# Two-layer hybrid block on one NeuronCore: last expert units one by one, scatter and output by column parts, ten constant products ahead of the ranks

## The reference

```python
g_sel = argmax(xt @ wg + bg)                       # 1 of 4 groups
top_v, top_i = top_k(e_logits[g_sel], 2)           # 2 of its 8 experts
gates = softmax(top_v) * g_gate
...
y[token] += gate * ((silu(xb @ w1[e]) * (xb @ w3[e])) @ w2[e])     # for each chosen expert e of 32
```

## Time and profile before

| | |
|---|---|
| median of 3 runs | 1458.95 us (1457.89 to 1459.53) |
| the profiled execution's own time | 1456.56 us |
| its span | 1454.7 us, 14458 instructions |
| TensorE products busy | 1142.2 us (79%) |
| VectorE, ScalarE, GpSimd busy | 326.3, 198.2, 43.7 us |
| moved by DMA | 477.99 MB, mean 329 GB/s |
| granted clock, mean | 0.909 of full speed |

### The profile page before, as it was taken

One profiled execution on the slowest core, in us unless ns is written; L12 is line 12 of the kernel. 1 busy time (PEld: TensorE's weight loads), 2 busy tenths in 40 slices (PEclk: granted clock), 3 DMA queues, 4 the chain that ended last, 5 costly groups with the idle time before them and its releaser, 6 DMA issues.

```text
span 1454.7 us, 14458 instructions
## 1 busy us (share of the span) xinstructions
PE 1142.2 (79%) x5962; PEld 563.6 (39%) x5962; DVE 326.3 (22%) x843; ACT 198.2 (14%) x468; POOL 43.7 (3%) x79
## 2 busy tenths in 40 slices
PE   8999998977768766685869999998866666666575
PEld 5775455543223222231325776465312212122121
DVE  1216543132021110110102286232201101011011
ACT  2024302210000010000002252131000000000000
POOL 0110000000000000000001100000000000000000
PEclk9999999979889898997989999998988888789888
DMA  9663373369999999999998355534999999999996
GB/s 368 217 232 116 114 284 123 116 243 418 426 425 428 427 423 427 427 427 425 428 409 319 116 174 207 199 116 173 403 427 428 426 427 426 427 427 428 427 427 264
DMA packets 94356, 477.99 MB, mean 329 GB/s; under 512 B 6390, under 2 KB 15054, under 8 KB 44878
## 3 DMA queue, kind: packets, MB, share of 16 engines
q1 hardware_dynamic: 93367, 475.25, 80.7%
...
...
## 4 chain that ended last, share of the span: by engine, by line
PE 54%; DMA 37%; DVE 4%; SPq 1%; ACT 1%; issue 1%; POOL 0%; DVEq 0%; ACTq 0%; POOLq 0%
PE bank L1445 51%; DMA ring<-exp_w 36%; PE bank L1452 2%; SPq L563 1%; DMA conv_mem<-memT 1%; DMA ring<-w_in 1%; ACT fox_ssd L746 0%; DVE SCO L1029 0%; DVE fox_ssd L1193 0%; DVE X L1038 0%; ACT H L897 0%; DVE proj_ht L976 0%; ACT SCO L742 0%; DVE proj_ht L997 0%; DVE Y L1284 0%
## 5 line engine op out<-in xcount | busy, mean ns | idle before, releaser
L1445 PE MATMUL bank<-ring,proj_ht 128*32 128x512 f32 (+3 forms) x2496 | 455.0, 673 | 153.4 <-DMA ring<-exp_w 150.8
L1445 PEld LDWEIGHTS bank<-ring,proj_ht 128*32 128x32 f32 (+1 forms) x2496 | 170.4, 142 | 393.8 <-issue 380.9
L1445 PE MATMUL bank<-ring,SCO 128*32 128x512 f32 x928 | 128.8, 690 | 67.4 <-DMA ring<-exp_w 58.4
L1038 DVE TENSOR_TENSOR X<-X,bank 128x512 f32<-128x512 f32 x64 | 44.0, 688 | 310.0 <-PE bank L1445 310.0
L1445 PE MATMUL bank<-ring,H 128*128 128x512 f32 x256 | 112.5, 593 | 0.0
L1445 PE MATMUL bank<-proj_ht,H 128*128 128x128 f32 x512 | 77.1, 304 | 28.4 <-DVE proj_ht L997 25.9
L1445 PEld LDWEIGHTS bank<-proj_ht,H 128*128 128x128 f32 x512 | 67.5, 209 | 67.3 <-DVE proj_ht L997 36.9
L1445 PEld LDWEIGHTS bank<-ring,SCO 128*32 128x32 f32 x928 | 35.4, 124 | 145.9 <-issue 133.6
L1029 DVE SCALAR_TENSOR_TENSOR SCO<-Y,bank 128x512 f32<-128x512 f32 x16 | 17.1, 1069 | 289.6 <-PE bank L1445 289.6
L1445 PE MATMUL bank<-fox_ssd,proj_ht 128*128 128x512 f32 x128 | 59.1, 604 | 17.8 <-ACT fox_ssd L746 17.8
L1445 PEld LDWEIGHTS bank<-ring,H 128*128 128x128 f32 x256 | 47.7, 190 | 55.6 <-issue 55.0
...
## 6 DMA issues: line engine op xcount, KB each, us to landing
ring<-exp_w SPq DMA_DIRECT2D x182, 2048.0 KB, 19.9
ring<-w_in SPq DMA_DIRECT2D x8, 2048.0 KB, 17.3
ring<-xa_wkv SPq DMA_DIRECT2D x4, 2048.0 KB, 10.0
ring<-w_out SPq DMA_DIRECT2D x4, 2048.0 KB, 9.5
ring<-xa_wq SPq DMA_DIRECT2D x4, 2048.0 KB, 9.6
ring<-xa_wo SPq DMA_DIRECT2D x4, 2048.0 KB, 7.7
ahead<-xa_wkv SPq DMA_DIRECT2D x4, 2048.0 KB, 28.1
...
```

The lines of the kernel that those rows point to most:

```text
L1038: last = v.tensor_tensor(x, x, bank[B_SCAT[i]][:, :], ALU.add)
L1445: return nc.tensor.matmul(dst, lhsT, rhs, start=start, stop=stop)
```

## The change

1. The host lays the 268 columns of `fv` out as one contiguous array `w_fv`; one load takes the place of two (the second brought the 8 columns of dt in pieces of 32 bytes).
2. Channel `c * 128 + p` of X now belongs to partition `p`, chunk `c` (before, channel `8 * p + c`), so that a chunk is a run of 128 columns. `w_in`, `xa_wq` and `xa_wkv` are read with that row order, and gains and the transposed memory are laid out by it. The input of the experts and router keeps the old order.
3. HT of layer input is made by column parts: parts of both tiles for columns 0 to 511, then 512 to 1023; banks 5 and 6 change places.
4. Ten products `ident` x `tri` of 256 columns go into the ranks' bank after the logits, in both layers; nobody reads them.
5. Down products of units 10 and 11: first all of column half 0, then half 1. In the last quad of a layer unit 10 is waited for and used alone, then unit 11. ScalarE copies each half when it is done.
6. Scatter and sums: half 0 of both tiles, then half 1, each with its own semaphore step. The output goes in four pieces of 128x512 instead of two of 128x1024.

```diff
@@ -121,7 +120,7 @@
-    jobs = two("hT1", 0) + two("hT1", 1)
+    jobs = [("hT1", t, i) for i in range(2) for t in range(NT)]
@@ -158,7 +157,7 @@
-PINNED = {("hT1", 0, 0): 2, ("hT1", 0, 1): 5, ("hT1", 1, 0): 6, ("hT1", 1, 1): 7, ("rank",): 5, ("total",): 7}
+PINNED = {("hT1", 0, 0): 2, ("hT1", 1, 0): 5, ("hT1", 0, 1): 6, ("hT1", 1, 1): 7, ("rank",): 5, ("total",): 7}
@@ -197,10 +196,12 @@
+N_IDLE = 10
...
+SCATTER = [(t, c) for c in range(2) for t in range(NT)]
@@ -444,6 +444,10 @@
+        def added(s, n, t, c):
+            return s.x_added, n * len(SCATTER) + SCATTER.index((t, c)) + 1
@@ -522,9 +526,9 @@
-                w = W_FV if kind == "fv" else w
-                rows = "(c p) n -> p c n" if kind in ("w_out", "wo") else "(p c) n -> p c n"
-                v = a[name][l].rearrange(rows, c=KC)
+                if kind == "fv":
+                    return w, a["w_fv"][l].rearrange("p (c n) -> p c n", c=KC)
+                v = a[name][l].rearrange("(c p) n -> p c n", c=KC)
@@ -542,11 +546,7 @@
-                place = ring_view(i % SLOTS, IN_COLS["fv"][1] if unit[0] == "fv" else w)
-                sp.dma_start(place[:, :, 0:w], src).then_inc(landed[i % SLOTS], 16)
-                if unit[0] == "fv":
-                    dt = a["w_in"][l].rearrange("(p c) n -> p c n", c=KC)[:, :, C_DT:C_DT + SH]
-                    sp.dma_start(place[:, :, w:], dt).then_inc(dt_in, 16)
+                sp.dma_start(ring_view(i % SLOTS, w), src).then_inc(landed[i % SLOTS], 16)
@@ -636,12 +636,13 @@
-            for t in range(NT):
-                sp.wait_ge(first.x_added, (DEPTH * NQ - 1) * NT + t + 1)
+            for t, c in SCATTER:
+                sp.wait_ge(*added(first, DEPTH * NQ - 1, t, c))
...
-                sp.dma_start(out[0, t * P:(t + 1) * P, :], X[:, t, :]).then_inc(x_out, 16)
-            sp.wait_ge(x_out, 16 * NT)
+                cols = slice(c * 512, (c + 1) * 512)
+                sp.dma_start(out[0, t * P:(t + 1) * P, cols], X[:, t, cols]).then_inc(x_out, 16)
+            sp.wait_ge(x_out, 16 * len(SCATTER))
@@ -741,10 +742,12 @@
-                act.wait_ge(*used(s, n, 12))
-                for i in range(2):
-                    last = nc.scalar.copy(YS[:, i * 512:(i + 1) * 512], bank[B_DOWN[i]][:, :])
-                last.then_inc(s.YS_ready, 1)
+                for c in range(2):
+                    if c == 0:
+                        act.wait_ge(s.down_half, n + 1)
+                    else:
+                        act.wait_ge(*used(s, n, MOE_UNITS))
+                    nc.scalar.copy(YS[:, c * 512:(c + 1) * 512], bank[B_DOWN[c]][:, :]).then_inc(s.YS_ready, 1)
@@ -1031,15 +1034,12 @@
-                for i in range(4):
-                    t, c = i // 2, i % 2
+                for i, (t, c) in enumerate(SCATTER):
...
-                    last = v.tensor_tensor(x, x, bank[B_SCAT[i]][:, :], ALU.add)
-                    if c == 1:
-                        last.then_inc(s.x_added, 1)
-                dve.wait_ge(s.x_added, n * NT + NT)
+                    v.tensor_tensor(x, x, bank[B_SCAT[i]][:, :], ALU.add).then_inc(s.x_added, 1)
+                dve.wait_ge(s.x_added, n * 4 + 4)
@@ -1052,8 +1052,9 @@
-                for t in range(NT):
-                    transposed_x("hT1", g_ch[:, G_X, :], t)
+                for i in range(2):
+                    for t in range(NT):
+                        gained(l, ("hT1", t, i), g_ch[:, G_X, 4 * i:4 * i + 4], HT[:, t, 4 * i:4 * i + 4, :])
@@ -1547,21 +1546,43 @@
-                for i in range(4):
-                    if i % 2 == 0:
-                        u = landed_rows(2, i // 2, 1024)
+                def down(u, experts, i, c):
+                    for e in experts:
+                        r = slice(CAP * e, CAP * (e + 1))
+                        last = mm(bank[B_DOWN[c]][r, :], HIDT[:, i, r],
+                                  u[e // 2][:, e % 2, i % 2, c * 512:(c + 1) * 512], start=i == 0, stop=i == 3)
+                    return last
+                u = landed_rows(2, 0, 1024)
+                for i in range(2):
...
-                        for e in range(QUAD):
-                            r = slice(CAP * e, CAP * (e + 1))
-                            last = mm(bank[B_DOWN[c]][r, :], HIDT[:, i, r],
-                                      u[e // 2][:, e % 2, i % 2, c * 512:(c + 1) * 512], start=i == 0, stop=i == 3)
-                    if i % 2 == 1:
-                        last.then_inc(s.units_used, 2)
+                        last = down(u, range(QUAD), i, c)
+                last.then_inc(s.units_used, 2)
+                if s is first and q == NQ - 1:
+                    u = []
+                    for pair in range(2):
+                        u.append(landed_unit(10 + pair, 1024))
+                        for c in range(2):
+                            for i in (2, 3):
+                                last = down(u, (2 * pair, 2 * pair + 1), i, c)
+                            if pair == 1 and c == 0:
+                                last.then_inc(s.down_half, 1)
+                        last.then_inc(s.units_used, 1)
+                else:
+                    u = landed_rows(2, 1, 1024)
+                    for c in range(2):
+                        for i in (2, 3):
+                            last = down(u, range(QUAD), i, c)
+                        if c == 0:
+                            last.then_inc(s.down_half, 1)
+                    last.then_inc(s.units_used, 2)
...
-                pe.wait_ge(s.YS_ready, n + 1)
-                for i in range(4):
-                    t, c = i // 2, i % 2
+                for i, (t, c) in enumerate(SCATTER):
+                    pe.wait_ge(s.YS_ready, n * 2 + c + 1)
@@ -1572,16 +1593,17 @@
-                def transpose_x(name, t):
-                    for i in range(2):
-                        transposes(l, (name, t, i), [dealt(t)[:, 4 * i + j, :] for j in range(4)])
-                for t in range(NT):
-                    if l == 0:
-                        pe.wait_ge(x_in[t], 16)
-                    else:
-                        pe.wait_ge(first.x_added, (l * NQ - 1) * NT + t + 1)
-                    transpose_x("hT1", t)
+                def transpose_x(name, t, i):
+                    chunks = [slice((4 * i + j) * P, (4 * i + j + 1) * P) for j in range(4)]
+                    transposes(l, (name, t, i), [X[:, t, c] for c in chunks])
+                for i in range(2):
+                    for t in range(NT):
+                        if l == 0:
+                            pe.wait_ge(x_in[t], 16)
+                        else:
+                            pe.wait_ge(*added(first, l * NQ - 1, t, i))
+                        transpose_x("hT1", t, i)
@@ -1837,17 +1865,20 @@
-                transpose_x("xT", 0)
+                transpose_dealt_x(0)
...
-                transpose_x("xT", 1)
+                transpose_dealt_x(1)
...
+                pe.wait_ge(*free(l, job))
+                for _ in range(N_IDLE):
+                    mm(bk(l, job)[:, 0:S], ident, tri[:, 0:S])
...
-                pe.wait_ge(*free(l, job))
@@ -1911,11 +1942,13 @@
-    gains = np.stack([g["norm1_g"], g["mem_norm_g"], g["norm2_g"]], axis=1).reshape(DEPTH, 3, P, KC)
-    arrays["gains"] = np.ascontiguousarray(gains.transpose(0, 2, 1, 3)).reshape(DEPTH, P, 3 * KC)
+    gains = np.stack([g["norm1_g"], g["mem_norm_g"], g["norm2_g"]], axis=1).reshape(DEPTH, 3, KC, P)
+    arrays["gains"] = np.ascontiguousarray(gains.transpose(0, 3, 1, 2)).reshape(DEPTH, P, 3 * KC)
+    w_fv = np.concatenate([g["w_in"][:, :, C_FV:C_DQK], g["w_in"][:, :, C_DT:C_DT + SH]], axis=2)
+    arrays["w_fv"] = np.ascontiguousarray(w_fv.reshape(DEPTH, KC, P, -1).transpose(0, 2, 1, 3)).reshape(DEPTH, P, -1)
...
-    arrays["memT"] = np.ascontiguousarray(g["mem"][0].T.reshape(P, KC, S))
+    arrays["memT"] = np.ascontiguousarray(g["mem"][0].T.reshape(KC, P, S).transpose(1, 0, 2))
```

17 lines of the change are left out of this document (9 added, 8 removed).

## The result

The changed kernel takes 1448.58 us (median of 5 runs, 1446.89 to 1449.37) where the kernel before, run beside it, takes 1457.89 (5 runs, 1454.33 to 1459.53). The ratio of the two kernels' runs is 0.9941, 95% interval 0.993 to 0.9953: 8.6 us less, 6.9 to 10.2. (The medians alone differ by 9.3.) The profiled execution took 1449.37 us, its span is 1447.5 (before 1454.7).

A forecast was written before the change was run, and what follows sets the result against it. Full DMA engines bound the expert streams, TensorE sets the pace outside them. Terms -1.1 - 0.7 - 0.6 - 0.6 + 0.2 - 2.9 = -5.7 us give 1450.9 (profiled execution) or 1453.2 (median); range 1448.8 to 1458.0.

The forecast's parts named there:

- the best bounds: All five places at their best bounds together: -9.8 us, from which the range was begun at 1448.8.
- a clock that is up early: Choice of experts: more gain than counted because the clock rises early, 1450 us; chance 0.05.
- step 3: Four xa_wkv loads in layer 0's full stream: new row order brings 426 GB/s for 425, -0.6 us (0 to -1.0).
- Step 1: Start: one load for two, first projection at 9.3 us for 10.40, -1.1 us (0 to -1.8).
- Step 2: Choice of experts: ten products raise the clock for the gathers but delay the ranks; net -0.7 and -0.6 us.
- Step 4: Last quad of layer 0: scatter 0.4 us sooner, VectorE's new order costs 0.62; +0.2 us (-0.4 to +1.1).
- Step 5: Last quad of layer 1 and output: scatter 2.5 us sooner, smaller last piece 0.4; -2.9 us (-1.6 to -3.1).
- Rival A: Choice of experts: late clock rise, the ten products' delay eats the gathers' gain; 1454.5 us, chance 0.2.
- B: Last quads: units one by one don't pay, +0.9 us in layer 0, +2 in layer 1; 1456.1, chance 0.1.
- C: Choice of experts: the ten products never raise the clock and ranks come late; slower, 1462.5 us, chance 0.03.
- D: Start: change not felt, parameters or following weights are waited for instead; 1454.3 us, chance 0.07.

The follow-up runs named there:

- N_IDLE = 0: The changed kernel without its ten products of constants; 1449.65 us, ratio 0.9956 to the kernel before.
- the ten alone: The kernel before with only the ten products of constants added, in both layers; 1454.85 us, ratio 0.9978.
- before 2: A second profiled execution of the kernel before, nothing changed; 1455.59 us, span 1453.8.

## Why the prediction was right, point by point

The forecast was 5.7 us less, the range 1448.8 to 1458.0, faster with 0.85. It is faster, by 8.6 us (6.9 to 10.2): half as much again as forecast. 1448.58 lies 0.2 us below the range; applied to the median of 1458.95 from which the forecast started, the ratio gives 1450.3, inside it. Two figures of the forecast don't follow from its own terms: the best bounds give 1458.95 - 9.8 = 1449.1 as the lower end, not 1448.8, and a clock that is up early gives 1453.2 - 2.2 = 1451.0, not 1450. By the stretches of profiled executions, step by step:

| step | forecast | measured | by |
|---|---|---|---|
| 1 start | -1.1 | -1.2 to -1.6 | two executions of before; the single load alone 1.0 |
| 2 ten products | -0.7, -0.6 | -0.7, -1.1 | N_IDLE = 0; -0.7, -1.0 by the ten alone |
| 3 row order in the stream | -0.6 | none that stands out | old row order |
| 4 end of layer 0 | +0.2 | +0.4 | stream to scatter 452.92 to 452.73; scatter to projection +0.6 |
| 5 end of layer 1, output | -2.9 | -3.3 | last unit to scatter -2.6, scatter to end -0.7 |

Together -5.9 to -6.3, with the signs and the order of the terms as forecast, save step 3. Read from before and after alone, the choices give -2.2 or -0.6 (layer 0, by the execution of before) and -1.0 for step 2.

- *Step 1* named the two that are late next rightly, load and HT. In this execution the projection starts at 8.83, right behind TensorE's last transposes for HT, and the load had landed sooner than the 9.3 forecast. In five of the ten profiled kernels with the single load the projection does wait for it, and starts between 8.85 and 9.34; so the two are nearly level.
- *Step 2* was right in its net and less so in its working, so the match of the net is partly luck. The rise came some 5.7 us after the start of the ten in layer 0, not 4.8, and the ten took 7.40 us, not 6.8. For that all behind the ranks ran at full clock: ranks to stream 8.61 us in both layers, for 12.0 and 11.2 before, so 3.4 and 2.6 us of gain and not 3.0 and 2.3. The price in layer 1 was as forecast: from logits to ranks 9.52 us for 7.92 in the kernel before, 1.6 later (forecast 1.7). In layer 0 it is 1.2 or 2.7 us (9.94 for 8.78, or 7.20 in before 2) around a forecast of 2.3. Set against the kernel without the ten but with the other edits, price and gain are both smaller: 1.2 and 1.0 of price, 1.8 and 2.1 of gain. What the ten buy is an earlier rise: from fall to rise the clock is at half for 13.7 us or more in the choices without them and for 6.8 with them.
- *Step 3* failed. It took 425 against 426 GB/s for a price of the strided rows. A load of the dense part does take 2 us more, but with the old order the full stream runs at 426, and the changed kernel's at 425. The 1 GB/s doesn't follow the row order, so pricing it was the step that failed. A landing time wasn't a rate.
- *Step 4* was right in kind. The scatter followed 0.2 us sooner behind the stream than before, not 0.4, and VectorE's order cost 0.60 (forecast 0.62). What it did not see is what the split is worth there: it was priced against a wait of 1.52 us as in the kernel before; but in the two executions with the ten and without the split TensorE waits 2.78 and 3.30 us and loses the clock, and with the rest of the change the stretch from the stream to the scatter is 1.7 us longer than with the split (454.41 for 452.73).
- *Step 5* was right: unit 11 in 3.63 us (forecast 3.44), the sums 0.86 apart, 10.4 us from the last landing to the end of the span (forecast 11, before 13.8). That TensorE would have no gap from 1431 on was wrong: it still stood 0.91 us before unit 11. The output gave 0.7, more than the 0.4 taken and than the bound of 0.6. The Trainium skill's rule (DMA: Bandwidth & Descriptors, Anatomy of one DMA), by which a piece of half the size saves its data time alone, gave 0.6, an estimate: the landing of one piece, 2.6 us before and 2.0 after, agrees with it, and the two pieces in the new order show 0.8. Its fixed part doesn't fit here: the page gives the 2.0 us for transfers issued from GpSimd, these come from SyncE, and of the 2.0 us in which 256 KB landed 0.6 are data at 425 GB/s, which leaves some 1.4.
- *Rival A* (the ten gain nothing) fell by N_IDLE = 0 and by the ten alone; *B* (units one by one don't pay) by the kernel without the split, and the pairs ran at full clock. The Trainium skill's rule on packs (TensorE: Matmul & The Clock Gate, Packing small matmuls) agrees with the runs: 16 records take 3.63 us in pairs and 1.92 in packs of four, both at full clock, so the time goes by the number of packs. *C* (the clock never rises) fell by the gathers in 2.05 us and a granted clock of 1.00 from 302 on; *D* (start not felt) by the projection at 8.83, though its microsecond is as small as what the dense part differs by from one execution to the next.

What stays open is some 2.3 us: the runs say 8.6, the terms add up to 6.3 at most. The lower end of the interval, 6.9, lies near. The profiled executions of before were faster than their medians and that of after slower than its own, so the missing part lies in executions that left no trace. If most executions of before had the longer choice of layer 0 (20.79 us for 19.19), 1.6 us of it would be found; no trace shows how often they had it.
